# An mLSTM stage: entering products grouped ahead of value products, modulation columns turned part by part, clears on GpSimd

## The reference, cut to what matters

```python
mx = jnp.split(silu(c) @ w_ada + b_ada, 6)      # and mc from c_ctx: "modulation"
# per head and direction, chunks of 128 tokens; b = cumsum(log_f)
a   = b + m_prev
m_t = max(a, max_s log_d)                       # log_d = b_t - b_s + log_i_s, s <= t
s   = (q k^T) * exp(log_d - m_t)
num = s @ v + exp(a - m_t) * (q @ C_prev)       # value products + entering products
den = sum(s) + exp(a - m_t) * (q . n_prev)
h   = num / max(|den|, exp(-m_t))               # both directions added, rms norm, times sigmoid(o)
```

## Time and profile before

| what | us |
|---|---|
| median of 3 runs (lowest, highest) | 2671.57 (2669.79, 2673.32) |
| profiled execution, its own time | 2666.56 |
| its span, first to last instruction | 2664.7 |
| the mlstm stage in it | 221.3 to 368.1 |
| end of `values(3)` in it, and start of the first part of the head loop | 346.66, 274.95 |
| end of `add_state(0)`, start of `values(0)` | 261.5, 276.82 |
| start of parts 0 to 3 | 228.1, 230.6, 233.1, 235.7 |
| mean granted TensorE clock | 0.932 of 2.4 GHz |

### The profile page before, as it was taken

The page is one execution under the profiler, slowest core; times in us unless marked ns, Lnnn a source line. Parts: engine busy times, 40 slices in busy tenths (PEclk is TensorE's granted clock), DMA queues, the critical chain, the costliest instruction groups (busy, mean ns, idle before and its releaser), DMA issues. The chain is left out here.

```text
span 2664.7 us, 30672 instructions
## 1 busy us (share of the span) xinstructions
PE 2415.6 (91%) x10732; PEld 1799.4 (68%) x10732; DVE 1541.2 (58%) x2421; ACT 1173.2 (44%) x1848; POOL 300.0 (11%) x217
## 2 busy tenths in 40 slices
PE   6997987689999999995499889999989988999997
PEld 2874576356767676763466667888867767788886
DVE  4975333367777777774745436746635554574573
ACT  4213234156666666663444434423424443342341
POOL 0001000011212121211034200000004420000000
PEclk8997567789999999997799999999999998999999
DMA  6303322169999999996432013232222201323222
GB/s 240 98 22 135 125 71 109 53 239 361 363 348 359 357 357 344 368 370 233 180 114 71 16 64 116 98 103 95 81 103 93 94 16 64 111 91 99 95 78 80
DMA packets 87009, 427.17 MB, mean 160 GB/s; under 512 B 19760, under 2 KB 19888, under 8 KB 51312
## 3 DMA queue, kind: packets, MB, share of 16 engines
q1 hardware_dynamic: 67600, 392.10, 41.0%
q0 software_dynamic: 19296, 33.60, 3.5%
HBM read 415.14 MB, written 38.80 MB: 170 GB/s over the span
## 5 line engine op out<-in xcount | busy, mean ns | idle before, releaser
L1719 DVE TENSOR_TENSOR w_gu_low<-raw,w_gu_high 128x1024 fp32r<-128x1024 f32 x264 | 322.8, 1224 | 121.8 <-ACT w_gu_high L1668 111.4
L1668 ACT ACTIVATE w_gu_high<-raw 128x1024 fp32r<-128x1024 f32 x264 | 279.8, 1060 | 108.6 <-PE banks L1624 107.8
L2619 PE MATMUL banks<-h_high,w_high 128*128 128x512 f32 x704 | 276.2, 392 | 12.5 <-DVE w_low L2719 12.5
L2619 PE MATMUL banks<-h_low,w_high 128*128 128x512 f32 x704 | 275.6, 391 | 0.0
L2619 PE MATMUL banks<-h_high,w_low 128*128 128x512 f32 x704 | 275.5, 391 | 0.0
L1636 PE MATMUL banks<-raw,act_t 128*128 128x512 f32 x528 | 237.6, 593 | 0.9 <-ACT act_t L1691 0.9
L1624 PE MATMUL banks<-w_gu_high,x_t_high 128*128 128x512 f32 x528 | 214.1, 405 | 2.0 <-DVE x_t_low L1726 2.0
L1624 PE MATMUL banks<-w_gu_high,x_t_low 128*128 128x512 f32 x528 | 208.0, 394 | 0.0
L1624 PE MATMUL banks<-w_gu_low,x_t_high 128*128 128x512 f32 x528 | 207.6, 393 | 0.0
L2646 ACT ACTIVATE w_high<-raw 128x2048 fp32r<-128x2048 f32 (+2 forms) x74 | 124.0, 1676 | 156.6 <-PE banks L2629 152.7
L2683 DVE TENSOR_TENSOR w_low<-raw,w_high 128x2048 fp32r<-128x2048 f32 (+2 forms) x74 | 148.3, 2004 | 58.9 <-ACT w_high L2646 58.7
(11 more groups left out here) (435 smaller groups left out, 4809.4 us busy)
## 6 DMA issues: line engine op xcount, KB each, us to landing
raw<-in_w_e SPq DMA_DIRECT2D x198, 1024.0 KB
raw<-in_w_up SPq DMA_DIRECT2D x42, 1024.0 KB
w_ada<-in_w_ada_later SPq DMA_DIRECT2D x16, 1024.0 KB
expert_rows<-y_rows SPq DMA_DIRECT2D x16, 1024.0 KB, 15.9
raw<-in_w_down SPq DMA_DIRECT2D x16, 768.0 KB
w_qkv<-in_w_even SPq DMA_DIRECT2D x7, 1536.0 KB
w_qkv<-in_w_odd SPq DMA_DIRECT2D x7, 1536.0 KB
w_in<-in_w_in SPq DMA_DIRECT2D x20, 512.0 KB
```

The costliest lines, as they stand in the source:

```text
L1668: act.activation(w_gu[c].high[:].rearrange("p j n -> p (j n)"), ex.chunk(c, s), ACT.Copy).then_inc(gu_high, 1)
L1719: dve.tensor_tensor(w_gu[c].low[:].rearrange("p j n -> p (j n)"), ex.chunk(c, s), w_gu[c].high[:].rearrange("p j n -> p (j n)").bitcast(F3 ...
L2619: mm = pe.matmul(ps[:, 2 * s + c, :], wp[:, at:at + P], hp[:, k, :], start=(k == 0 and i == 0), stop=(k == KT - 1 and i == 2))
```

## The change

Six things change, all in `mlstm`.

1. `values(h)` issues all eight entering products first and then all eight value products; it waits for `finish(h-1)` bank by bank.
2. Part n's row is turned into columns right ahead of part n+1's matmuls (`turn_part`), into the upper half of bank 7; the product always uses the lower half. Only the last turn is left for the end.
3. TensorE's order: three parts instead of four ahead of the row matmuls, which signal `r` and `a` apart; part 3 after them; `spread_g` and `products` run a head earlier; both parts of a head follow `values(h)`.
4. VectorE computes `scores` of head h+1 ahead of `finish(h)`.
5. The clears move to GpSimd; its `so` multiplies move into the head loop.
6. Setup order: `leave` and `dec` first, then `enter` and `g`; ScalarE makes the `w` exponents ahead of `e`, and `r_sb` lies in another tile so that `w_rows` may be cleared and written apart from it. `keep_row(3)` comes after the copy of `a`, `keep_row(4)` after the copies of the first states.

The core of the diff:

```diff
 # TensorE
 def later_part(n):
     pe.wait_ge(aw_in[n % SLOTS], 16 * (n // SLOTS) + 16)
     if n >= 1:
-        pe.wait_ge(row_copied, n)
+        turn_part(n - 1)
...
+def turn_part(n):
+    pe.wait_ge(row_copied, n + 1)
+    for a in range(2):
+        at = MOD_AT + 4 * n + 2 * a
+        mm = pe.matmul(ps[:, B_ADA, at:at + 2], ada_row(n)[:, a * P:(a + 1) * P], CONST.of(m.const, "quarters"), start=True, stop=True)
+    return mm
 def values(h):
     pe.wait_ge(sp_done, 2 * h + 2)
-    if h >= 1:
-        pe.wait_ge(h_done, h)
     for i in range(TT):
+        if h >= 1:
+            pe.wait_ge(h_done, TT * (h - 1) + i + 1)
         for r in range(2):
-            to = ps[:, i, r * ONE:(r + 1) * ONE]
-            pe.matmul(to, qe[...], state[...], start=True, stop=False)
-            mm = pe.matmul(to, sp_sb[...], m.v[...], start=False, stop=True)
+            pe.matmul(ps[:, i, r * ONE:(r + 1) * ONE], qe[...], state[...], start=(r == 0), stop=False)
+    for i in range(TT):
+        for r in range(2):
+            mm = pe.matmul(ps[:, i, r * ONE:(r + 1) * ONE], sp_sb[...], m.v[...], start=False, stop=(r == 1))
...
-later_part(5)
+later_part(4)
 pe.wait_ge(qe_done, 4)
+add_state(1)
 spread_g(0)
 pe.wait_ge(dec_copied, 1)
 spread_g(1)
 pe.wait_ge(cols_done, 1)
 products(0)
-add_state(1)
 pe.wait_ge(st0_copied, 1)
 add_state(2)
-later_part(6)
+later_part(5)
 pe.wait_ge(c_done, 1)
 add_state(3)
-later_part(7)
+for n in (2, 3):
+    spread_g(n)
+for n in (6, 7):
+    later_part(n)
+products(1)
 pe.wait_ge(c_done, 3)
 for h in range(H_M):
-    if h + 1 < H_M:
-        spread_g(2 * h + 2)
-        spread_g(2 * h + 3)
-    later_part(8 + 2 * h)
     values(h)
-    later_part(9 + 2 * h)
-    if h + 1 < H_M:
-        products(h + 1)
-pe.wait_ge(row_copied, N_LATER)
...
+    for n in (8 + 2 * h, 9 + 2 * h):
+        later_part(n)
+    if h + 2 < H_M:
+        spread_g(2 * h + 4)
+        spread_g(2 * h + 5)
+        products(h + 2)
+turn_part(N_LATER - 1).then_inc(parts_done, 1)
 # VectorE, head loop
         exponent(2 * h + 3)
-    finish(h)
-    if h + 1 < H_M:
         scores(2 * h + 2)
         scores(2 * h + 3)
+    finish(h)
 # ScalarE, setup
-for n in range(4):
+for n in range(3):
     keep_row(n)
...
+act.wait_ge(a_made, 1)
 act.activation(a_sb[:], ps[0:ROWS_N, B_A, :], ACT.Copy).then_inc(a_copied, 1)
-act.wait_ge(bounds_done, 1)
-for c in range(TT):
-    ins = act.activation(e_rows[...], g[...], ACT.Exp, bias=enter[:, c:c + 1])
+keep_row(3)
+act.wait_ge(leave_done, 1)
```

More of the change, by code:

```diff
@@ L709, in mlstm @@
         most, r0 = sb("running_most", [ROWS_N, SEQ]), sb("ctx_most", [ROWS_N, 1])
-        w_rows, r_sb, e_rows, gm = sums[0][0:ROWS_N], sums[1][0:ROWS_N], most, a_up
+        w_rows, e_rows, gm = sums[0][0:ROWS_N], most, a_up
         enter, leave, dec = sb("most_before", [ROWS_N, TT]), sb("most_upto", [ROWS_N, TT + 1]), sb("decay_rows", [ROWS_N, TT])
@@ L768, in _ @@
             def _(pool):
-                for i in range(TT):
-                    pool.tensor_tensor(m.so[:, i, :], m.so[:, i, :], ROWV.of(m.rowv, "norm_g"), ALU.mult).then_inc(so_done, 1)
+                pool.memset(sums[0][:], 0.0)
+                pool.memset(sums[1][:], 0.0).then_inc(cleared, 1)
+                pool.memset(zero[:], 0.0)
+                pool.memset(enter[:], 0.0)
+                pool.memset(leave[:], 0.0)
+                pool.memset(most[:], 0.0).then_inc(cleared, 1)
                 pool.wait_ge(g_done, 1)
+                pool.wait_ge(bounds_done, 1)
                 pool.wait_ge(a_copied, 1)
                 pool.tensor_tensor(gm[:], g[:], a_sb[:], ALU.subtract).then_inc(gm_done, 1)
+                for i in range(TT):
+                    pool.wait_ge(sp_done, 2 * i + 2)
+                    pool.tensor_tensor(m.so[:, i, :], m.so[:, i, :], ROWV.of(m.rowv, "norm_g"), ALU.mult).then_inc(so_done, 1)
             @block.scalar
@@ L785, in keep_row @@
                     act.wait_ge(aw_used, n + 1)
-                    act.activation(ada_row(n), ps[:, B_ADA, HALF * (n % 2):HALF * (n % 2) + HALF], ACT.Copy).then_inc(row_copied, 1)
+                    act.activation(ada_row(n), ps[:, B_ADA, 0:HALF], ACT.Copy).then_inc(row_copied, 1)
                 def decays(n):
@@ L797, in square @@
                 def square(h):
[L798 removed]
+                    act.wait_ge(h_done, TT * h + TT)
                     if h >= 1:
@@ L822, in _ @@
                 act.activation(dec[:], dec[:], ACT.Exp).then_inc(dec_exp, 1)
+                act.wait_ge(bounds_done, 1)
+                for c in range(TT):
+                    ins = act.activation(e_rows[:, tokens(c)], g[:, tokens(c)], ACT.Exp, bias=enter[:, c:c + 1])
+                ins.then_inc(e_done, 1)
                 act.wait_ge(w_turned, 1)
@@ L835, in _ @@
                 ins.then_inc(st0_copied, 1)
+                keep_row(4)
                 keep_row(5)
@@ L860, in _ @@
                 dve.tensor_tensor(tmp[:], lsig[:], m.gates[:], ALU.max).then_inc(l_abs, 1)
[L861 to L864, removed]
+                dve.memset(m.v[:, :, :, DV:ONE], 1.0)
+                dve.wait_ge(cleared, 1)
                 for t in sums:
                     dve.tensor_copy(t[32:48], m.gates[:])
[L867 to L870, removed]
+                dve.wait_ge(cleared, 2)
                 dve.wait_ge(l_ln, 1)
@@ L885, in _ @@
                 own(dve, dve.tensor_tensor_scan(most[bw, ::-1], r_sb[bw, SEQ - 1::-1], zero[bw, :], r0[bw, :], ALU.max, ALU.add))
[L886 to L889, removed]
+                dve.tensor_scalar(leave[:, TT:TT + 1], r0[:], -1.0, None, ALU.mult)
+                dve.tensor_scalar(leave[fw, 0:TT], most[fw, P - 1:SEQ:P], -1.0, None, ALU.mult)
+                own(dve, dve.tensor_scalar(leave[bw, 0:TT], most[bw, 0:SEQ:P], -1.0, None, ALU.mult))
+                dve.sem_inc(leave_done, 1)
                 dve.tensor_copy(enter[fw, 0:1], r0[fw, :])
@@ L892, in _ @@
                 dve.tensor_copy(enter[bw, TT - 1:TT], r0[bw, :])
[L893 to L896, removed]
+                own(dve, dve.tensor_copy(enter[bw, 0:TT - 1], most[bw, P:SEQ:P]))
+                dve.tensor_tensor(dec[:], enter[:], leave[:, 0:TT], ALU.add).then_inc(dec_made, 1)
+                dve.wait_ge(a_copied, 1)
+                own(dve, dve.tensor_scalar(a_up[:], a_sb[:], -M_LEAST, None, ALU.add))
+                dve.scalar_tensor_tensor(g[:], most[:], -1.0, a_up[:], ALU.mult, ALU.min).then_inc(g_done, 1)
                 dve.wait_ge(g_done, 1)
                 dve.sem_inc(bounds_done, 1)
-                dve.tensor_tensor(dec[:], enter[:], leave[:, 0:TT], ALU.add).then_inc(dec_made, 1)
                 def weigh(r, first, n):
@@ L1039, in values @@
                     pe.wait_ge(sp_done, 2 * h + 2)
-                    if h >= 1:
-                        pe.wait_ge(h_done, h)
                     rows = slice(QK * (h % 2), QK * (h % 2) + QK)
                     for i in range(TT):
+                        if h >= 1:
+                            pe.wait_ge(h_done, TT * (h - 1) + i + 1)
                         for r in range(2):
-                            to = ps[:, i, r * ONE:(r + 1) * ONE]
-                            pe.matmul(to, qe[rows, h // 2, r, tokens(i)], state[rows, h // 2, r, i, 0:ONE], start=True, stop=False)
-                            mm = pe.matmul(to, sp_sb[(2 * h + r) % 4][:, tokens(i)], m.v[:, i, h, 0:ONE], start=False, stop=True)
+                            pe.matmul(ps[:, i, r * ONE:(r + 1) * ONE], qe[rows, h // 2, r, tokens(i)], state[rows, h // 2, r, i, 0:ONE],
+                                      start=(r == 0), stop=False)
+                    for i in range(TT):
+                        for r in range(2):
+                            mm = pe.matmul(ps[:, i, r * ONE:(r + 1) * ONE], sp_sb[(2 * h + r) % 4][:, tokens(i)], m.v[:, i, h, 0:ONE],
+                                           start=False, stop=(r == 1))
                     mm.then_inc(pv_done, 1)
@@ L1059, in _ @@
                 pe.wait_ge(run_done, 1)
-                for name, bank, cols in (("r", B_RC, slice(SEQ, ALLT)), ("r", B_RX, slice(0, SEQ)), ("a", B_A, slice(0, SEQ))):
+                for name, bank, cols, done in (("r", B_RC, slice(SEQ, ALLT), None), ("r", B_RX, slice(0, SEQ), r_made), ("a", B_A, slice(0, SEQ), a_made)):
                     for r in range(2):
@@ L1063, in _ @@
                                        start=(r == 0), stop=(r == 1))
-                mm.then_inc(r_made, 1)
-                later_part(4)
+                    if done is not None:
+                        mm.then_inc(done, 1)
+                later_part(3)
                 pe.wait_ge(r_copied, 1)
```

31 lines of the change are left out of this document (12 added, 19 removed).

## The result

The changed kernel takes 2624.82 us, the median of 4 runs (2624.24 to 2627.25), against 2670.68 us before: a ratio of 0.9831, 95% interval 0.9814 to 0.9848, 45.9 us faster. I had forecast 2647 us and a range from 2631 to 2664.

What follows compares the result with a forecast made beforehand. The prediction took PE's list of work to bound the head loop. Its terms, +0.9 + 1.8 + 2.0 - 10.3 - 14.9 - 4.1 = -24.6 us, gave 2642.0 profiled and a median of 2647 us, range 2631 to 2664.

Steps and rivals of the forecast that it cites:

- Part 1: Head loop, values in two groups: a pass takes 7.6 us instead of 11.62, four times, -16.1 us at 1.2 GHz.
- Part 2: The head loop's other work: loop of 59.5 us against 69.8, so -10.3 us with the clock unchanged.
- up through the loop: Bound for the clock at 2.4 GHz throughout the head loop: 30.6 us, -28.9.
- part 3: Before the loop, from add_state(0)'s end to values(0): 17.2 us against 15.4, +1.8, with ACT's waits hidden by 2.5 us.
- the +2.0: Ahead of the loop: the clock rises 4 us late, each us costing half a us; bounds 0 and +14.
- part 4: Setup, up to add_state(0): clock stays down, start at 258.95 against 258.10, +0.9 us; with the clock up, -4.9.
- Part 5: The end, from values(3) to the next stage: +17.3 instead of 21.4 us, -4.1; at 2.4 GHz -6.9.
- part 6: The clock, largest unknown: up for a third of the loop's time, -14.9 us; later rise ahead of it, +2.0.
- rival B: The clock stays up from 261 on, through the loop and end: -43.4 us, 2628 us; chance 0.12.
- Rival A: The clock stays at 1.2 GHz in the loop: -11.7 us, 2660 us; chance 0.20.
- C: The clock misses its rise at add_state(0), staying down until the loop's end: +2.3 us, 2674 us; chance 0.07.
- D: Weight loads do not run ahead in the loop's grouped passes: +6.4 us, 2678 us, slower; chance 0.04.

Runs made afterwards that it cites:

- one kernel above: Changed kernel with keep_row(3) behind the exponents and the turns of parts 0 to 2 moved to where PE waits for the w exponents: 2622.45 us.
- 8.75 in another: Changed kernel with all sixteen turns of modulation columns at the end again, after the last part: 2627.44 us.
- one form without groups: Kernel before, alternating order kept, entering products widened from 64 rows to 128, so the output differs: 2624.94 us.
- grouped passes that began at 1.2 GHz: Kernel before with only values(h) grouped, plus 24 useless two-column products ahead of each pass: 2671.88 us, one run.
- the alternating one: Changed kernel with one edit undone, values(h) alternating again between 64-row and 128-row products: 2646.98 us, ten runs from 2634.09 to 2677.18.
- the groups alone: Kernel before with only values(h) edited: its eight entering products, then its eight value products: 2626.8 us.
- two shortened setup chains: Changed kernel with keep_row(3) behind the exponents, 2628.15 us; the same with turns of parts 0 to 2 moved to PE's exponent wait, 2622.45 us.
- the changed setup: Changed kernel with keep_row(3) and the turns of parts 0 to 2 moved later, plus useless 128x128 products in PE's setup waits: 2614.26 us against 2624.87.

## Why the prediction was off

By its own parts, against the profiled executions:

| part | forecast us | measured us |
|---|---|---|
| setup, to `add_state(0)` | +0.9 | +1.5 |
| prelude, to `values(0)` | +1.8 + 2.0 | +2.4 |
| loop | -10.3 - 14.9 | -39.5 |
| end | -4.1 | -7.1 |
| sum | -24.6 | -42.7 |

Part 1, the groups, was right in mechanism and size: 7.46 us at 1.2 GHz against 7.6, 3.9 at 2.4. Part 2, the loop's list, came out as far as a warm loop can tell: the bound "up through the loop" was 30.6 us, and the loop took 30.39. The waits I had followed in part 3 were hidden as said; the clock rose at 265.3 there, in a spread, 4.6 us after the start of `add_state(0)` for 3.0 before, so the +2.0 was too much by 1.4. In part 4 the clock stayed down through the row matmuls, which took 8.74 us for 4.48 before, as assumed. That was in part luck: one list of work led to 4.48 us in one kernel above and to 8.75 in another. The setup began part 0 at 8.1 us, 1.3 later than I had put it, for want of its weights, and `add_state(0)` came 0.6 us later than forecast. (The terms that part 4 lists behind 252.05 add up to 257.95 and not 258.95; the turn of the w rows, 0.66 us, is not among them.) GpSimd's clears took 0.5 to 1.1 us each for the large ones and delayed nothing. Part 5 came out at the value worked for 2.4 GHz, -6.9 against -7.1.

The step that failed is part 6: "I take it up for a third of the loop's time". The clock was at 2.4 GHz for all of it, so the term was not -14.9 but -29.1 (59.5 - 30.4, the first of the two being my own sum for the loop at 1.2 GHz). Its premise, "fall again in the spreads", failed: no spread in the loop took the clock down. The size of both ends was right and rival B held the case, with 0.12, too little. What I had missed in the rows is that before, from 261 to 275, the clock stayed up through spreads and gaps of up to 0.79 us. The loop was cold because the clock fell just ahead of it and none of the four alternating passes raised it again. Three runs bear that out: useless full-array work ahead of each pass raised the clock, and it stayed at 1.00 in spite of the breaks; one form without groups raised it within a pass; grouped passes that began at 1.2 GHz raised it at their end. The other term of the loop, PE's list at 1.2 GHz, explains the remaining 10.3 us by that same sum (4 x (11.62 - 7.46) = 16.6 from the groups, less the turns and waits moved in).

Rival A (clock down), C (no rise ahead of the loop) and D (weight loads don't run ahead) did not occur; D's price is refuted by the 7.46 us. What stays open: why one list of work leads to a fall of the clock in one execution and not in another. The kernel before ranged from 2638.85 to 2678.31 over the experiments' own runs of it, the alternating one over 43 us, and one of the four runs with the groups alone took 2640.44. That such runs differ by the clock is on record (in the last case 0.938 against 0.943 to 0.944); where in the stage they differ is not.

## What to carry to other kernels

Order matmuls so that the row form changes seldom: a change cost 0.30 us at 1.2 GHz and 0.2 at 2.4, and a pass with sixteen changes did not bring the clock back once it had fallen, which was worth more than the breaks. When a stage is bound by PE at a granted clock of 0.50 though it counts as busy, ask first what would raise the clock, before shortening any chain: here one regrouped loop gave what six edits gave. Of two shortened setup chains, one reached `add_state(0)` 3.6 us sooner and lost 3.4 behind it at the lower clock; the other reached it 10 us sooner, but 4.7 of that were the clock's, and 3.5 were lost again. And where the clock can fall, take several runs of each kernel and set their mean granted clocks beside their times: one profile shows one of the courses that it can take. If the work at hand can't be made dense, full-array filler can pay: 23 us ahead of the alternating passes in the kernel before, and 10.6 us in PE's waits in the changed setup, reordering included.

## What the runs showed of the hardware

- Adding 32 useless 128x128 products to the kernel before made it 23 us faster (2647.54 against 2670.3).
- 48 records of weight loads with two columns, back to back, let the granted clock fall from 1.00 to 0.50 within them, with PE 4.00 us busy of 4, in four heads of four.
- TensorE busy in 69.85 of 69.85 us with alternating forms left the granted clock at 0.50 for all of it.
- The same list of matmuls was followed by a fall of the granted clock in one execution (279.8, the changed kernel alternating) and by none in another (the changed kernel).
- A change between 64-row and 128-row matmuls costs about 0.2 us at 2.4 GHz as well: a product every 0.42 us against 0.22 with one form. At the higher clock an alternating pass (6.69 us) is still slower than a grouped one (3.9).
- In the changed kernel the granted clock stayed at 1.00 for the whole loop, through 36-row spreads and waits of 0.6 us. In the setup of the kernel before, two such spreads (3.76 us) ran at 0.50 and did not raise it.
